# Neighbourhood attention in a float32 trunk: query blocks of 8 rows by 16 columns in place of 2 rows by 64, fewer and smaller score tiles, and another layout of bias, keys and values

## What is computed

```
def row_block(r):                       # one row of 64 queries
    r0 = jnp.clip(r - kr // 2, 0, rows - kr)          # kr = 8 key rows
    k_win = k_band[:, :, :, col_idx]                  # 16 key columns around each query
    s_win = einsum(q_r, k_win) * scale + bias[None]   # learned 2-D relative bias
    s_ctx = einsum(q_r, k_ctx) * scale                # 256 context keys
    p = softmax(concatenate([s_win, s_ctx], axis=-1))
    return p_win @ v_win + p_ctx @ v_ctx
```

## Time and profile before

| | |
|---|---|
| median of 3 runs | 3200.53 us (3199.91 to 3201.78) |
| time of the profiled execution, and its span | 3199.34 us, 3197.5 us |
| PE busy | 2978.2 us, 93% |
| DVE, ACT, POOL busy | 55%, 25%, 23% |
| share of PE in the chain that ended last | 77% |
| granted TensorE clock, mean | 0.974 |

### The profile page before, as it was taken

The page is one execution under the profiler, slowest core; times in us unless marked ns, Lnnn a source line. Parts: engine busy times, 40 slices in busy tenths (PEclk is TensorE's granted clock), DMA queues, the critical chain, the costliest instruction groups (busy, mean ns, idle before and its releaser), DMA issues.

```text
span 3197.5 us, 44615 instructions
## 1 busy us (share of the span) xinstructions
PE 2978.2 (93%) x15738; PEld 2467.4 (77%) x15738; DVE 1762.4 (55%) x2975; ACT 814.8 (25%) x1425; POOL 737.0 (23%) x457
## 2 busy tenths in 40 slices
PE   5899999689999999999969899999798999999996
PEld 1588888478888888888759788888675888888884
DVE  1645545666666776655551366666614554555556
ACT  1311111321111111111142366666623111111112
POOL 0221111021111111111111254445421222222210
PEclk8899999899999999999989999999998999999998
DMA  9210013021222212211035556555630111111111
GB/s 356 73 53 26 32 46 89 0 69 55 76 72 74 79 55 78 69 44 39 33 95 123 166 144 177 161 160 144 182 138 26 39 52 46 40 59 39 59 39 59
DMA packets 156872, 269.26 MB, mean 84 GB/s; under 512 B 70272, under 2 KB 97920, under 8 KB 156800
## 3 DMA queue, kind: packets, MB, share of 16 engines
q1 hardware_dynamic: 156800, 268.32, 26.8%
HBM read 222.13 MB, written 50.07 MB: 85 GB/s over the span
## 4 chain that ended last, share of the span: by engine, by line
PE 77%; DVE 6%; issue 5%; ACT 4%; DMA 4%; SPq 1%; POOL 1%; DVEq 0%; POOLq 0%; ACTq 0%
PE psum L668 42%; PE psum L699 19%; PE psum L828 4%; PE psum L807 3%; PE psum L882 2%; PE psum L851 2%; PE psum L865 2%; DMA o_dram<-o_st_lo 1%; DVE residual L1343 1%; DVE prod L1323 1%; DMA mod_raw<-mod_panels 1%; PE psum L634 1%; POOL w_lo L1657 1%; ACT squares L982 1%; ACT pt_hi L1158 1%
## 5 line engine op out<-in xcount | busy, mean ns | idle before, releaser
L1343 DVE SCALAR_TENSOR_TENSOR residual<-psum,modulation,residual 128x512 f32<-128x512 f32 (+1 forms) x1072 | 718.2, 690 | 884.5 <-PE psum L699 882.5
L1657 POOL TENSOR_TENSOR w_lo<-raw,w_hi 128x1024 fp32r<-128x1024 f32 x196 | 491.2, 2520 | 1927.9 <-ACT w_hi L976 1925.0
L668 PE MATMUL psum<-act_hi,w_hi 128*128 128x512 f32 (+1 forms) x2208 | 589.2, 367 | 9.5 <-POOL w_lo L1657 7.5
L668 PE MATMUL psum<-act_lo,w_hi 128*128 128x512 f32 (+1 forms) x2208 | 589.3, 367 | 0.0
L668 PE MATMUL psum<-act_hi,w_lo 128*128 128x512 f32 (+1 forms) x2208 | 588.7, 367 | 0.0
L668 PEld LDWEIGHTS psum<-act_hi,w_hi 128*128 128x128 f32 x2208 | 397.7, 188 | 88.3 <-issue 7.7
L976 ACT ACTIVATE w_hi<-raw 128x1024 fp32r<-128x1024 f32 x196 | 204.1, 1061 | 1013.8 <-PE psum L668 938.1
L668 PEld LDWEIGHTS psum<-act_lo,w_hi 128*128 128x128 f32 x2208 | 380.2, 188 | 70.7
L668 PEld LDWEIGHTS psum<-act_hi,w_lo 128*128 128x128 f32 x2208 | 380.3, 188 | 70.5
L699 PE MATMUL psum<-prod_hi,w_hi 128*128 128x512 f32 (+1 forms) x1072 | 408.3, 381 | 28.2 <-DVE residual L1343 10.4
L699 PE MATMUL psum<-prod_hi,w_lo 128*128 128x512 f32 (+1 forms) x1072 | 396.3, 370 | 0.0
(11 more groups left out here) (120 smaller groups left out, 3707.4 us busy)
## 6 DMA issues: line engine op xcount, KB each, us to landing
raw<-ffn_panels SPq DMA_DIRECT2D x132, 512.0 KB, 5.0
mod_raw<-mod_panels SPq DMA_DIRECT2D x48, 512.0 KB, 9.6
mod_in<-mod_rest SPq DMA_DIRECT2D x64, 384.0 KB, 3.1
raw<-conv_panels SPq DMA_DIRECT2D x32, 512.0 KB, 5.2
k_hi<-k_dram SPq DMA_DIRECT2D x32, 320.0 KB, 5.7
k_lo<-k_dram SPq DMA_DIRECT2D x32, 320.0 KB, 7.3
v_st<-v_dram SPq DMA_DIRECT2D x32, 320.0 KB, 7.2
raw<-qk_panels SPq DMA_DIRECT2D x16, 512.0 KB, 4.4
```

What stands on the lines that cost most here:

```text
L668: mm = pe.matmul(psum[:, bank + b, 0:tn], w[:, s, kb, :], acts[h][:, kb, t0:t0 + tn], start=(kb == 0 and n == 0), stop=(kb == KB - 1 and n ...
L1343: dve.scalar_tensor_tensor(out=residual[:, ob, t0:t0 + tn], in0=psum[:, 6 + r % 2, 0:tn], scalar=modulation[:, gates + ob, kind_of(t0):kin ...
L1657: pool.tensor_tensor(panel(w_lo, s), raw[:, s], panel(w_hi, s), ALU.subtract).then_inc(lo_done[s], 1)
```

## The change

- A block is 8 rows by 16 columns of queries. Its keys are a window of 12 rows by 32 columns (384 keys) and the context: 640 scores for each block. `scores` makes 4 products of 384 columns and 4 of 256 in a unit, both blocks at one place. The band scores of the two blocks have banks 0 and 1, their context scores share bank 2, and `values` alternates between banks 3 and 6.
- Every unit has three groups: two of 4 turned blocks, one of 2. The third has products of 128 columns, one key tile for one block. A pair has 24 groups, and the chunks are dealt anew.
- The bias table of a head is 2 x 3 x 384 entries for each of the 128 queries of a block, already masked, 9216 bytes a partition. All 16 are built in DRAM during the convolution: first 32 transfers of 576 KB fill them with the masked value (`blank`), then six stages load relative rows, POOL masks them, and 16 transfers store them. POOL's `tables` goes.
- The values of a unit are gathered by four transfers of 64 KB (pieces of 512 bytes) into one of eight tiles, each loaded after its last use, and those of the context once a head; before, a head came in two transfers.
- High and low parts of queries, keys and outputs are stored by one transfer in place of two; `o_st` has two buffers by `u % 2`. Queries are stored in the order of the column blocks, and after `wo` the sums are added to the residual by two instructions of 256 columns instead of one of 512.

```diff
-        GROUPS = [OUTER, INNER, INNER, OUTER]
+        SLOTS_OF = [[(0, 1, ((0, BAND + P), (1, BAND))), (2 * P, 2, ((0, BAND + 2 * P), (1, BAND + P)))],
+                    [(4 * P, "c0", ((0, C0), (1, C0))), (6 * P, "c1", ((0, C1), (1, C1)))],
+                    [(8 * P, 0, ((0, BAND),)), (9 * P, 3, ((1, BAND + 2 * P),))]]
...
-        QK_CHUNKS = {**chunks(1, 2, 0, (5, 5, 5, 5, 4)), **chunks(1, 3, 6, (6, 6, 6, 6)), **chunks(1, 4, 11, (8, 8, 8)),
-                     **chunks(2, 0, 15, (5, 5, 5, 5, 4)), **chunks(2, 1, 21, (5, 5, 5, 5, 4))}
-        QK_DRAINED = {6: (1, 2), 11: (1, 3), 15: (1, 4), 21: (2, 0), 27: (2, 1)}
+        QK_CHUNKS = {**chunks(1, 2, 0, (8, 8, 8)), **chunks(1, 3, 4, (8, 8, 8)), **chunks(1, 4, 8, (12, 12)),
+                     **chunks(2, 0, 11, (6, 6, 6, 6)), **chunks(2, 1, 16, (5, 5, 5, 5, 4))}
+        QK_DRAINED = {4: (1, 2), 8: (1, 3), 11: (1, 4), 16: (2, 0), 22: (2, 1)}
...
+            sp.wait_ge(pool_step, 9)
+            for h in range(HEADS):
+                for ab in range(2):
+                    sp.dma_start(bias_dram[h, :, ab], blank[:]).then_inc(bias_filled, 16)
+            for j in range(1, KB):
                 for s in range(4):
                     load_panel("conv", s, j, conv_panels[j, s])
+                if j == 2:
+                    sp.wait_ge(bias_filled, 16 * 2 * HEADS)
+                if 0 <= j - 2 < BIAS_STAGES:
+                    store_bias_rows(j - 2)
+                if j - 1 < BIAS_STAGES:
+                    load_bias_rows(j - 1)
...
+            def load_v(i, u):
+                b, j = divmod(u, COL_BLOCKS)
+                at_least(sp, pv_ready, UNITS * i + u + 1 - UNITS)
...
+                for r in range(KEY_ROWS):
...
+                    sp.dma_start(v_band[b][j][r * WINDOW:(r + 1) * WINDOW].bitcast(F32), src).then_inc(v_in[u], 16)
...
             load_heads(0, 0)
-            load_v(0, 0)
+            for u in range(4):
+                load_v(0, u)
             store_qk(1, 0)
...
+                at_least(pe, s_done, 16 * i + 2 * u)
+                j = u % 4
+                q0 = ab * BANK + j * P
+                for part in range(2):
+                    rows = k_st[:, b, part, 0:TL].rearrange("p (r c) -> p r c", c=GRID_W)
+                    pe.matmul(psum[:, ab, 0:BAND_KEYS], q_st[:, b, q0:q0 + P],
+                              rows[:, EDGE * ab:EDGE * ab + BAND_ROWS, WINDOWS[j]:WINDOWS[j] + WINDOW],
+                              start=(part == 0), stop=(part == 1))
+                for part in range(2):
+                    mm = pe.matmul(psum[:, CTX_BANK, ab * TC:(ab + 1) * TC], q_st[:, b, q0:q0 + P], k_st[:, b, part, TL:T],
+                                   start=(part == 0), stop=(part == 1))
                 mm.then_inc(s_ready, 1)
...
-                        if g < 2:
-                            if u + 2 < UNITS:
-                                scores(i, u + 2, g)
-                            elif not last:
-                                scores(i + 1, u + 2 - UNITS, g)
+                        if g == 1:
+                            for ab in range(2):
+                                if u + 2 < UNITS:
+                                    scores(i, u + 2, ab)
+                                elif not last:
+                                    scores(i + 1, u + 2 - UNITS, ab)
                         fill(i, group0[u] + g, reach)
...
-                at_least(act, o_out, 32 * (UNITS * i + u))
+                at_least(act, o_out[u % 2], 16 * (UNITS // 2 * i + u // 2))
...
-                dve.wait_ge(s_ready, n + 1)
+                dve.wait_ge(s_ready, 16 * i + 2 * u + 2)
```

More of the change, by code:

```diff
@@ L130, in trunk @@
         assert nxt <= weight_at, (nxt, weight_at)
[L133 to L139 removed]
+        probs, nxt = place("probs", [P, 4, KEYS], F32, residual_at)
@@ L140, in trunk @@
+        PT = 2 * P * 5
+        pt_hi, nxt = place("pt_hi", [P, PT], F32R, nxt)
+        pt_lo, nxt = place("pt_lo", [P, PT], F32R, nxt)
+        neg_s, nxt = place("neg_s", [P, 2, KEYS], F32, nxt)
+        bias_0, nxt = place("bias_0", [P, 2, COL_KINDS, BAND_KEYS], F32, nxt)
+        V_PIECE = 4 * ROW_TILES * P
+        v_at = [nxt + V_PIECE * n for n in range(3)]
+        assert v_at[-1] + V_PIECE <= act_at, (v_at, act_at)
         q_st, nxt = place("q_st", [P, 2, TL], F32R, raw_end - SPARE_SLOTS)
@@ L520, in _ @@
             store_qk(1, 1)
+            for u in range(4, UNITS - 1):
+                load_v(0, u)
             def attention(i, panels=True, heads=True, queries=True):
@@ L565, in attention @@
                     load_o(3)
-                if not heads:
+                store_o(i, 5)
+                if heads:
+                    load_v(i + 1, 5)
+                else:
                     sp.wait_ge(s_ready, 2 * UNITS * PAIRS)
@@ L921, in _ @@
             pe.wait_ge(v_lo_done, 4 * TOK_TILES + 4)
[L922 removed]
+            pe.wait_ge(attn_consts, 2)
             turn(0, 0, 0)
@@ new lines, in _ @@
+            first, inner, last = (col_mask[:, kind, :] for kind in range(COL_KINDS))
+            keep_where(first[:, 0:half], HEAD_GROUP * half + HEAD_GROUP - 1, HEAD_GROUP, -1)
+            keep_where(inner, HEAD_GROUP - 1, HEAD_GROUP, -1)
+            keep_where(last[:, 0:WIN_COLS], HEAD_GROUP - 1 - HEAD_GROUP * half, HEAD_GROUP, -1)
+            pool.wait_ge(pool_step, 2 + 3)
+            keep_where(first[:, WIN_COLS:WINDOW], -HEAD_GROUP * (WIN_COLS - half + 1), -HEAD_GROUP, 1)
+            keep_where(inner, HEAD_GROUP * (WIN_COLS - 1), -HEAD_GROUP, 1)
@@ L1652, in _ @@
+            keep_where(last[:, WIN_COLS + half:WINDOW], -HEAD_GROUP, -HEAD_GROUP, 1)
+            pool.wait_ge(pool_step, 2 + 6)
             pool.wait_ge(consts, CONSTS)
@@ L1676, in conv_step, with mask_bias_rows @@
                 split_lo("conv", 3, j)
+            def mask_bias_rows(n):
+                pool.wait_ge(bias_in, 16 * Q_COLS * (n + 1))
+                mask = col_mask[:, n % COL_KINDS, :][:, None, :]
+                pool.tensor_tensor(bias_stage[:], bias_stage[:], mask.to_broadcast([P, REL, WINDOW]),
+                                   ALU.add).then_inc(bias_masked, 1)
             conv_step(0)
-            with pool.Fori(1, KB - 1) as j:
+            for j in range(1, KB - 1):
                 conv_step(j)
+                mask_bias_rows(j - 1)
             conv_step(KB - 1, last=True)
```

412 lines of the change are left out of this document (197 added, 215 removed).

## The result

The changed kernel takes 3209.1 us (median), before 3200.5: ratio 1.0027, interval 1.0018 to 1.0035. The prediction was 3154, in a range of 3136 to 3188. The profiled execution of the changed kernel has a span of 3207.0 us; the same mark in both traces, read off one after the other, shows where the 9.5 us come from and where the forecast 46.4 went. An output mark is an ACT `o_st` (`out_high`), one a unit; the traces have 64.

A forecast was written before the change was run, and what follows sets the result against it. Six of eight pairs were taken as bound by PE's work; terms -37.6 - 1.4 - 18.4 + 4 + 6 + 1 = -46.4 on 3199.3 gave 3152.9, or 3154 us as a median, range 3136 to 3188.

The forecast's parts named there:

- PE's work in a full pair, 54.6: Full attention pair: PE's projections, scores and groups sum to 54.6 us, 7.3 less than before.
- the term of waits: Full pair: the 3.8 us of waits stay, and 1.0 is added for the last three groups without a chunk.
- Rival (b): Six pairs: transfers or drains hold the loop; late keys or outputs cost 3 to 4 a pair, 3176; chance 0.12.
- Its bandwidth half: Full pair: added value and bias transfers fill the DMA engines; occupation alone decides only under 85 GB/s for the values.
- The 59.4 of the pair: Full pair: work and waits together take 59.4 us, 6.3 less than before; six pairs give -37.6.
- all drains exposed by 1.4 more in two places: Six full pairs: the lower bound of the gain, -21 us in place of -37.6.
- The units without chunks, -18.4: Last 12 units, end of pair 6 and pair 7: shorter loop and smaller store stall bring them to 64.5 us.
- the loop term: Unit of pair 7: its loop over DVE and ACT falls from 6.18 to 5.6 us.
- 2 us for a store that is still late: End of pair 6: with two staging buffers the late store of outputs costs 2 us, against 12.93.
- Start of the attention, +4: Attention's start: later key store, bias ahead of the first query store, merged stores and waiting for both blocks; 0 to +10.
- Convolution, +6: Convolution step 1: its panels queue behind the fill, so the gate copies come at 164.8 instead of 158.9.
- In the later steps ... I cost them at nothing: Later convolution steps: 32 small transfers and a wait for POOL between panels cost nothing; without cover 5 us a step.

The follow-up runs named there:

- c1: Changed kernel with the fill behind step 1's first three panels, query/key stores ahead of values and bias, and output loads moved into pair 7: 3157.0 us, 0.9864.
- e2: Changed kernel with all stores of queries and keys issued by SP ahead of the value and bias transfers: 3177.1 us, 0.9927.
- d2: Changed kernel with only the stores of key tiles 3 and 4 issued ahead of the value and bias transfers of their block: 3185.3 us, 0.9956.
- c2: c1 with three chunks of projections begun one group later: 3140.3 us, 0.9823.
- e4: Changed kernel with the output projection's loads of outputs moved from pair 6 into pair 7, one behind each store: 3198.6 us, 0.9997.
- d5: c2 with three panels issued ahead of each bias stage's transfers and POOL's mask waiting for the step's three `prod_lo`: 3141.5 us, 0.9815.
- d1: c2 with POOL's mask waiting until DVE has done the three `prod_lo` of the same convolution step: 3147.1 us, 0.9832.
- d3: c2 with each merged store of queries and keys split again into two transfers, high and low part: 3146.1 us, 0.9832.
- c3: c1 with POOL's mask cut to the first staged bias row (32 columns in place of 480), all transfers kept: 3149.9 us, 0.9848.
- d4: c2 with the panels of slots 0 to 2 of the next convolution step issued ahead of a bias stage's 32 transfers: 3143.2 us, 0.9820.

## Why the prediction was wrong, step by step

**PE's work in a full pair, 54.6:** right (55.3 busy in a pair of c1; the same kind of sum gave 61.9 for 63.5 busy before). The step that failed is the term of waits, "I keep the 3.8, since the same five tiles are drained through one bank", with 1.0 added: 4.8 a pair forecast, and 63.2 - 54.6 = 8.6 measured. I priced the drains by bank and product count, and left out that the store between two drains is now issued behind four value transfers and a bias load of 1.18 MB. That costs 20 to 23 us in six pairs: against c1, in which e2's edit cured it, 10.3 of waits and 12.6 of PE at a lower clock behind them (d2 shows which stores they were). Rival (b) gave it 3 to 4 a pair with a chance of 0.12, for "keys or outputs that land late"; the mechanism and the price were right, the chance was far too low. Its bandwidth half is refuted. One of its sums was off: the other transfers take 38 us there, so the occupation would reach the pair's 59.4 with the values at about 110 GB/s; 85 is where it reaches the old 65.7.

**The 59.4 of the pair** came about in d2, e2 and c1 once SP's order let it, but in part by luck. The 3.8 was no wait of the drains: PE's idle time before was 2.2 a pair, 0.6 of it at the drains and 1.5 for `o_sum`, and the rest of the 3.8 is the difference between the sum and the busy time. After the change the 1.5 are gone, I take it by the alternating value bank, which I had called worth little (no run tests it alone); in their place c1 has 2.9 a pair at the drains and 1.15 for `probs`:

```profile
PE psum L897 <- DVE stage L1562: 17.3, 12, 1.6
PE psum L935 <- POOL probs L1766: 6.9, 6, 1.1
```

Those 2.9 are the place of the chunks, as c2 shows; the forecast had such a term ("all drains exposed by 1.4 more in two places") as its lower bound alone.

**The units without chunks, -18.4:** the loop term was right (5.78 for 5.6); "2 us for a store that is still late" was wrong. I took two staging buffers as a cure for a store that took 12.9 to land, without asking what stands ahead of it; it took 22.5 to land, and ACT waited 15.7 for it. e4 shows the loads of outputs to be 12.3 us of the 12 units; with e2's edit as well (3.1 alone) c1 gets 15.5. ACT's waits for stores there are then 2.2, and 12 units take 66.2 (d5) to 70.5 (d1) in the kernels with c1's order, 64.5 forecast.

**Start of the attention, +4:** +6.5 from the first staged tile to the first turned block. The later issue was right (16 value transfers in 8.7 us); wrong was that the store, as it comes later, lands so much faster: 5.97 in place of 8.74, a gain of 2.8 and not 5.7. The five merged stores were to give back 2.2 and gave nothing (d3). The first one takes 1.6 more to land (7.91; before the change 6.33), less than the 3.6 taken. The first output comes another 3.6 later. That is no wait: PE is busy without a gap from the first turned block to the first output in both, but at another granted clock (before, then after):

```profile
1811.97:1823.41 11.44, 11.44 (x78) 10.39 (x79) 7.46 (x24) 6.72 (x13) 6.90 (x6) 1.00 0.36 139
```

```profile
1827.69:1842.68 14.99, 14.99 (x77) 13.32 (x78) 6.30 (x19) 6.46 (x15) 2.55 (x4) 0.80 0.47 119
```

From these figures I estimate 3.0 us for the clock (a fifth of 14.99), and 0.6 for the work itself, which has 25 products of 512 columns in place of 20, as the chunks are larger. c1 has 14.22 us at 0.85.

**Convolution, +6:** right for the fill (5.4). "In the later steps ... I cost them at nothing" was wrong by 7.1 us at the end of the convolution. I had named the cost without cover as 5 us a step for ACT's split; the split was late and harmless, but the POOL instruction behind it moved beside DVE's products, and the mask beside `prod_lo`. Of the 0.9 to 1.1 a step, 0.7 is the mask (17.9 and 17.2; c3, d1, d5), and 0.2 to 0.4 the late `w_lo` together with it (40.8 to 41.0 and 40.6; taken away by c3 and by d4 alike).

**The rest.** Of the 12.5 us at the end of the convolution 4.0 come back up to the feed-forward part with no work changed, at another granted clock (before, then after):

```profile
562.27:662.60 100.33, 68.54 (x278) 44.16 (x277) 59.42 (x90) 42.27 (x76) 11.56 (x9) 0.85 0.00 0
```

```profile
574.75:671.09 96.34, 63.98 (x278) 41.00 (x277) 59.34 (x90) 42.26 (x76) 11.55 (x9) 0.92 0.00 1
```

c2 has 96.4 there and d5 100.6; single profiles differ by this, so marks behind that stretch are no better than 4 us. Behind the last unit 5 us more are lost, 3.1 of them before the output projection's long block starts; c1 keeps 2.6 of the 3.1. I didn't test this apart, and its cause stays open.

The rule of the Trainium skill that I had set aside ("DMA: Bandwidth & Descriptors", Where 436 GB/s comes from: the HBM side binds at about 358 GB/s) does not hold for these stores: 401 GB/s over the 48 us of the fill.

**In one line:** the terms of work were within 0.2 us a unit, and the large terms of waiting failed in the same way: I costed each new transfer by its bytes or its issue, not by what stands behind it in SP's queue (the mask and `w_lo` beside DVE are the exception). c1, whose only edits are SP's order, runs at 3157, three from the forecast. That nearness is partly luck: c1 no longer pays the +6 of the fill that the forecast had counted, and its later units and last stretch take more than forecast. c2 at 3140 is 59 us faster than the kernel before in the same comparison. No run made SP's edits on the kernel before, which also had stores of outputs at the end of pair 6 that took 6.1 and 12.9 us to land; how much of c1's 42 us is the new blocks and how much the order stays open.

## What to carry to other kernels

When a change adds transfers to a queue that is issued in order, write down for each place what is issued next, who waits for it, and when; a small store that frees a buffer goes ahead of loads that are needed a unit later. Make that list before pricing bytes: here the same bytes in another order were worth 50 us. Read the waits that a forecast keeps by their releaser, and not as what a sum leaves over. Price a stall of PE at about twice its length where the clock is at its upper level before it and falls behind it, as it did here; and test an edit again when another wait has been taken away, since it can be worth more.

## What the runs showed of the hardware

DVE and POOL slow each other. `prod` over 128x1282 takes 1.55 us alone and 3.46 to 3.48 beside POOL's `w_lo`; three `prod_lo` take 1.61 alone, 2.65 beside the mask; the mask takes 1.22 alone (d5), 1.4 beside `prod_lo` and 2.47 beside `prod`. They take turns: in six of the traces the tap product that meets a `w_lo` (40 times in the convolution) ends 1.35 us after the end of that `w_lo`, whether it starts 0.1 or 1.5 us behind it. One merged store of 2 x 256 KB lands 3.05 us after its issue, the second of two single stores 2.3. With a stall of 2.4 to 3.3 us in each pair the mean granted clock is 0.96 over six pairs; in c1, whose longest waits are 1.4 and 1.6 us, it is 1.00. Products of 128 columns start 0.10 us apart.
